# Two transformer blocks in float32 on one core: expert weights given back and loaded by halves for fourteen of sixteen pairs, with three changes of order

## The reference

```
x = x + hybrid_mixer(rmsnorm(x))            # mLSTM branch and spatial gating, one w_in of 10248 columns
x = x + memory_cross_attention(rmsnorm(x), rmsnorm(mem))     # w_xq, w_xkv, w_xo
x = x + hierarchical_moe(rmsnorm(x))        # 32 experts, each token goes to 2:
    hb = silu(xb @ w1[e]) * (xb @ w3[e])    #   w1, w3: 1024 x 512
    y  = hb @ w2[e]                         #   w2: 512 x 1024
x = rmsnorm(x)
# second block: modulation vectors from silu(c) @ w_ada (1024 x 6144), Hyena branch,
# differential attention over x and ctx, SwiGLU with 2816 hidden columns
```

## Time and profile before

| | |
|---|---|
| median of 3 runs | 1299.24 us (1298.53 to 1300.81) |
| the profiled execution | 1300.37 us, span 1298.6 us |
| mean granted TensorE clock | 0.998 of full speed |
| PE busy | 1261.2 us, 97% of the span |
| DVE, ACT, POOL busy | 698.1, 509.3, 102.9 us |
| moved | 362.89 MB, 279 GB/s over the span |

### The profile page before, as it was taken

The page is one execution under the profiler, slowest core; times in us unless marked ns, Lnnn a source line. Parts: engine busy times, 40 slices in busy tenths (PEclk is TensorE's granted clock), DMA queues, the critical chain, the costliest instruction groups (busy, mean ns, idle before and its releaser), DMA issues.

```text
span 1298.6 us, 17828 instructions
## 1 busy us (share of the span) xinstructions
PE 1261.2 (97%) x7053; PEld 887.4 (68%) x7053; DVE 698.1 (54%) x1169; ACT 509.3 (39%) x778; POOL 102.9 (8%) x111
## 2 busy tenths in 40 slices
PE   8999999999999999999999999999999999999998
PEld 7987886976776444444445444449966787899986
DVE  5675668667664323322322222247996868855552
ACT  5556674345244111111111111137344685644442
POOL 6740200200000000000000000000043000000000
PEclk9999999999999999999999999999999999999999
DMA  9654747958876999999999999995416254655440
GB/s 350 240 193 140 251 151 262 371 180 292 308 283 238 402 424 426 426 427 428 429 428 427 425 429 427 427 397 199 154 65 221 104 201 140 194 167 169 184 162 33
DMA packets 103316, 362.89 MB, mean 279 GB/s; under 512 B 4306, under 2 KB 28373, under 8 KB 89600
## 3 DMA queue, kind: packets, MB, share of 16 engines
q1 hardware_dynamic: 99872, 352.60, 70.0%
q0 software_dynamic: 3168, 9.06, 2.2%
q10 hardware_dynamic: 192, 0.06, 0.0%
HBM read 360.65 MB, written 1.05 MB: 279 GB/s over the span
## 4 chain that ended last, share of the span: by engine, by line
PE 85%; DVE 7%; ACT 3%; issue 2%; DMA 1%; POOL 1%; ACTq 0%; DVEq 0%; POOLq 0%
PE bank L544 37%; PE bank L955 17%; PE bank L975 8%; PE bank L929 5%; PE bank L1330 5%; PE bank L1006 3%; DVE ring_parts L1378 2%; PE bank L965 1%; ACT ring_parts L2211 1%; DMA ring<-in_w_xkv 1%; PE bank L633 1%; PE bank L956 1%; PE bank L1170 1%; PE bank L598 1%; PE bank L831 1%
## 5 line engine op out<-in xcount | busy, mean ns | idle before, releaser
L1378 DVE TENSOR_TENSOR ring_parts<-ring,ring_parts 128x1024 fp32r<-128x1024 f32 x202 | 243.6, 1227 | 128.7 <-ACT ring_parts L2211 125.8
L2211 ACT ACTIVATE ring_parts<-ring 128x1024 fp32r<-128x1024 f32 x222 | 230.0, 1057 | 189.6 <-PE bank L544 164.7
L544 PE MATMUL bank<-ring_parts,arena_parts 128*128 128x512 f32 x1056 | 272.3, 393 | 4.1 <-ACT ring_parts L2211 1.5
L544 PEld LDWEIGHTS bank<-ring_parts,arena_parts 128*128 128x128 f32 x1056 | 196.6, 188 | 48.6 <-ACT ring_parts L2211 2.8
L544 PE MATMUL bank<-arena_parts,ring_parts 128*128 128x256 f32 x1504 | 199.4, 285 | 3.0 <-DVE ring_parts L1378 1.8
L955 PE MATMUL bank<-ring,arena 128*64 128x512 f32 x432 | 190.6, 594 | 8.2 <-issue 8.2
L956 PE MATMUL bank<-ring,arena 128*64 128x512 f32 x448 | 197.9, 595 | 0.0
L544 PEld LDWEIGHTS bank<-arena_parts,ring_parts 128*128 128x128 f32 x1504 | 191.4, 193 | 5.1 <-issue 3.3
L955 PEld LDWEIGHTS bank<-ring,arena 128*64 128x64 f32 x432 | 57.5, 137 | 126.7 <-issue 126.7
L2494 ACT ACTIVATE arena<-bank 128x512 f32<-128x512 f32 x32 | 19.1, 597 | 227.4 <-PE bank L956 227.4
L975 PE MATMUL bank<-ring,arena 128*64 128x512 f32 x416 | 106.3, 596 | 0.0
(11 more groups left out here) (411 smaller groups left out, 1502.1 us busy)
## 6 DMA issues: line engine op xcount, KB each, us to landing
ring<-in_w SPq DMA_DIRECT2D x70, 2048.0 KB, 20.9
ring<-in_w_in SPq DMA_DIRECT2D x27, 2048.0 KB, 9.7
ring<-in_w_ada SPq DMA_DIRECT2D x12, 2048.0 KB, 8.7
flank<-in_w SPq DMA_DIRECT2D x12, 2048.0 KB, 21.1
ring<-in_w SPq DMA_DIRECT2D x22, 1024.0 KB, 9.9
ring<-in_w_ffn_gate SPq DMA_DIRECT2D x11, 1024.0 KB, 5.3
ring<-in_w_ffn_up SPq DMA_DIRECT2D x11, 1024.0 KB, 8.0
ring<-in_w_ffn_down SPq DMA_DIRECT2D x5, 2048.0 KB, 7.7
```

What stands on the lines that cost most here:

```text
L544: mm = pe.matmul(ps[:, o:o + width], *pair, start=(o == 0 and kk == 0 and ha + hw == 0), stop=(kk == kn - 1 and (ha, hw) == terms[-1] and ...
L1378: dve.tensor_tensor(low, src, high, ALU.subtract).then_inc(low_ready, 1)
L2211: act.activation(high, src, ACT.Copy).then_inc(high_ready, 1)
```

## The change

Four edits:

1. `HALF_PAIRS` becomes 14: units 7 to 90 are given back and loaded by halves, where it was units 7 to 18.
2. The down product of a pair that is given back by halves (`down_by_rows`, new) has the rows outside: each of the four blocks of rows is read for both halves of the columns before the next, so half the rows have been read in the middle. Both banks are then finished at the end.
3. In the first block's memory keys: `xkv0` is loaded before `ada3`; PE makes `xk0` straight after `ada_sum(1)`, with `ada_sum(2)` between its first two quarters, then `ada_part(3)`, then `xk1` with `ada_sum(3)` between its first two quarters. DVE makes `xkv0`'s first low part amid the products of spatial gating, and the last low parts of the activations (`split_activations(mem_parts, actT, (1, 3))`) ahead of `ada(0)` and `ada(1)`. ACT's list follows.
4. In front of `xq0`: the second tile's transposition (`turn(xT, ..., tiles_of=(1,))`) comes before `ada_part(6)` and `ada_sum(4)`.

```diff
@@ weight_units @@
-    ada_units(0, 4)
-    for j in range(4):
+    ada_units(0, 3)
+    whole("xkv0", cols(w["w_xkv"][0], 0))
+    ada_units(3, 4)
+    for j in range(1, 4):
         whole(f"xkv{j}", cols(w["w_xkv"][0], 512 * j))
@@ -375,7 +377,7 @@
-        HALF_PAIRS = 2
+        HALF_PAIRS = PAIRS - 2
@@ -747,11 +749,18 @@  PE
             ada_part(2)
             ada_sum(1)
+            memory_arrived = halves_split(12)
+
+            def summed(j, arrived=None):
+                def between(q):
+                    if arrived is not None:
+                        arrived(q)
+                    if q == 1:
+                        ada_sum(j)
+                return between
+            split_features("xk0", "xkv0", mem_parts, summed(2, memory_arrived))
             ada_part(3)
-            ada_sum(2)
-            split_features("xk0", "xkv0", mem_parts, halves_split(12))
-            ada_sum(3)
-            split_features("xk1", "xkv1", mem_parts)
+            split_features("xk1", "xkv1", mem_parts, summed(3))
@@ -787,9 +796,9 @@  PE
             ada_part(5)
+            turn(xT, hat2, hats=4, tiles_of=(1,))
             ada_part(6)
             ada_sum(4)
-            turn(xT, hat2, hats=4, tiles_of=(1,))
             ada_sum(5)
@@ -968,6 +977,9 @@  PE, down(n)
                 reach(pe, moe["hid"], 2 * n + 2)
+                if halved(n):
+                    down_by_rows(n, w2u)
+                    return
                 for half in range(2):
...
+            def down_by_rows(n, w2u):
+
+                for half in range(2):
+                    reach(pe, moe[f"low{half}"], n)
+                for k in range(KF):
+                    for half in range(2):
+                        for j in range(2):
+                            mm = pe.matmul(PS[4 + half][j * C:(j + 1) * C, :], hidT[:, j, k, :],
+                                           w2u[j][:, k, half * 512:(half + 1) * 512], start=(k == 0), stop=(k == KF - 1),
+                                           skip_group_check=True)
+                        if k == KF - 1:
+                            mm.then_inc(moe["down"], 1)
+                        elif half and k == KF // 2 - 1:
                             mm.then_inc(moe["half"], 1)
@@ -1587,12 +1612,13 @@  DVE, after each tile of the spatial gating's products
+                if t == 0:
+                    split_low(1)
+
+            split_activations(mem_parts, actT, (1, 3))
             dve.wait_ge(s["G_ready"], 8)
             ada(0)
             ada(1)
-            split_low(1)
-            split_activations(mem_parts, actT, (1, 3))
             split_low(3)
             ada(2)
@@ -2364,10 +2390,11 @@  ACT
             split_activations(memT, mem_parts, actT, (0, 2, 1, 3))
+            split_high(2)
             ada(2)
-            split_high(2)
+            split_high(4)
             ada(3)
-            split_high(2 + 12)
+            split_high(10)
```

More of the change, by code:

```diff
@@ L977, in down @@
                                            skip_group_check=True)
-                        if half and k == KF // 2 - 1 and halved(n):
+                    mm.then_inc(moe["down"], 1)
[9 more added lines that the diff above has]
+                        if k == KF - 1:
+                            mm.then_inc(moe["down"], 1)
+                        elif half and k == KF // 2 - 1:
                             mm.then_inc(moe["half"], 1)
-                    mm.then_inc(moe["down"], 1)
             def down_by_pieces(n):
```

## The result

The changed kernel takes 1311.95 us (median of 4, 1311.50 to 1314.26) beside 1299.84 for the kernel before: 1.0096 of it, 95% interval 1.0081 to 1.0112. The forecast was 1309.2; the median lies at the upper edge of its range. The profiled execution takes 1311.89 us, 11.5 more than the one of before.

A forecast was written before the change was run, and what follows sets the result against it. It took PE, busy 97%, as the bound, with transfers pacing later expert pairs. Expert stage +3.3, memory keys +6.5 and the transposition +0.2 made +10.0 on 1300.37, 1310.4; less 1.1 for the median, 1309.2 us; range 1302 to 1312.

The forecast's parts named there:

- What bounds the stage: Expert stage: later pairs run at the transfers' speed; rival that places were the limit: 1295.6 us, chance 0.06.
- Rate of the halves: Expert stage: halves cost 0.056 us more per unit, +4.0 us for 72 more units.
- The Trainium skill's rule: Expert stage: 1 MiB halves over 128 partitions lose no bandwidth, sum +6.0, 1305.2 us; rival, chance 0.14.
- Order of the halves: Expert stage: first of two units complete 2.5 us later, PE late by 0 to 1.0 at the end: +0.5 us.
- Rows outside: Pair 0's down product: signal 1.8 us earlier closes the idle DMA between 436 and 444 us: -1.2 us.
- Memory keys: First block: PE waits for banks ahead of xk0 and xv0, clock falls after each: 1.6 + 3.2 + 1.7 = +6.5 us.
- The rival by which the banks don't hold PE: Memory keys: no bank waits, the reordering gives -2.0 us; sum +1.5, 1300.7 us; chance 0.11.
- Edit 4: Ahead of xq0: xq0 waits slightly longer for xT1's bank, +0.2 us (-0.4 to 0.6).
- The step from the profiled execution to the median: Whole kernel: the median lies 1.1 us below the profiled execution, taking 1310.4 to 1309.2 us.

The follow-up runs named there:

- e9: Kernel before with only units 7 to 90 given back and loaded by halves, down products as before: 1304.21 us, ratio 1.0034.
- e10: Kernel before with units 19 to 90 each loaded as two 1 MiB transfers by columns, once the whole place is free: 1305.50 us, ratio 1.0036.
- e12: Kernel before with units 19 to 90 loaded by one 2 MiB transfer each, in 8 KB pieces mixing two experts' weights: 1306.13 us, ratio 1.0043.
- e3: Kernel before with only the rows-outside down product, halves for two pairs as before: 1298.58 us, ratio 0.9983.
- e1: Kernel before with units 7 to 90 by halves and the rows-outside down product, nothing else: 1303.71 us, ratio 1.0028.
- e5: Changed kernel with takes renumbered so xk0, xk1, xv0 and adaB3 get the banks of the kernel before: 1305.24 us, ratio 1.0035.
- e4: Kernel before with only the second tile's transposition moved ahead in front of xq0: 1301.18 us, ratio 1.0008.
- e2: Kernel before with only the reordered memory keys: 1307.84 us, ratio 1.0058.
- e6: Kernel before with the reordered memory keys, takes renumbered to keep the old banks: 1300.67 us, ratio 1.0003.
- e7: e6 with xkv0's second low part made earlier, ahead of the activations' last low parts: 1298.81 us against the kernel before, ratio 0.9985.
- e8: e7 with the rows-outside down product in the first two pairs, halves for two pairs as before: 1295.76 us, ratio 0.9961 to the kernel before.

## Where the prediction failed, and what of it held

Its direction and its account of where the time goes held. Two steps of the sum failed. The rate of the halves was mis-sized: +4.0 us forecast, 5.3 to 5.5 measured, which leaves the expert stage at +4.3 for +3.3. And the last step, 1.1 us off from the profiled execution to the median, had nothing to stand on.

- *What bounds the stage* (transfers, not places): right. Share 1.01 throughout, the waits ahead of `up` grew, and earlier issue brings nothing: e9, which issues first halves in the middle of a product where e10 waits for its end, has as long a stage (5.4 us longer than before, e10 5.3 without its stretch at half clock).
- *Rate of the halves, 72 x 0.056 = +4.0:* right in kind, mis-sized; this is the step that failed. 0.46 us a pair is 0.077 a unit, 5.5 for 72; by the stage it is 5.3 (e10) and 5.4 (e9). It was extrapolated from ten landings, read to 0.1 us: over 22.3 us that alone is 1.6 us in 72 units, and I took the middle. That the shorter rows are the cause was no part of the forecast; e12 shows it. The Trainium skill's rule (DMA: Bandwidth & Descriptors, Rules for kernel authors), under which the term would be nothing, is off by a little over 1% here: 421 to 422 GB/s for halves of 1 MiB over 128 partitions, 427 for whole loads.
- *Order of the halves, +0.5:* too much. e9 less e10 leaves 0.1, and that rests on taking 1.7 off for a stretch at half clock. It made up for 0.4 of the term above.
- *Rows outside, -1.2:* right: -1.4 (e3) and -1.2 (e1 beside e9), and where it was put, at 436 us.
- *Memory keys, +6.5:* right. Both banks hold PE (e5), for 3.41 and 3.05 us where 3.4 and 3.2 were forecast, and the clock falls behind both. Of the 7.0 us ahead of the stage, 6.5 are left when e4's 0.5 is taken off, and e2's stage starts 6.5 later. By the medians edit 3 alone costs 0.58%, 7.5 us (5.7 to 9.2). The rival by which the banks don't hold PE counted on a gain of 2.0 (its own sum, 0.1 + 1.5 - 3.5, gives 1.9): e6, with the old banks, gains nothing, since its wait is longer and the clock falls behind it.
- *Edit 4, +0.2:* 0.5 (e4's trace), inside its bounds, and by the bank that was named; by the medians 1.0 (-0.1 to 2.2), which isn't clear of no change.
- *The step from the profiled execution to the median, -1.1:* this failed too, by 1.2. The profiled execution of the changed kernel is its median (1311.89 and 1311.95). The one of before is 1.1 above a median of three; 66 more executions, run beside the experiments, have the median 1300.26, only 0.1 below it. They differ with the clock: the 27 with a mean granted clock of 0.999 or more have the median 1299.47, the other 39 have 1300.66, and the profiled one (0.998) has a stretch at half clock that not all have (below). An offset of that kind isn't handed on to another kernel.

The median is 2.75 us above the forecast: this 1.2, and 1.5 between the profiled executions (11.5 for 10.0), of which 1.0 are in the expert stage, 0.3 in edit 4, 0.4 ahead of everything that was changed and -0.2 behind the stage.

## What to carry to other kernels

Where the transfers set the pace, giving a place back sooner lands nothing sooner (it gained 1.2 to 1.4 us once, at 436 us, where the engines had run out of loads), and cutting rows in two to do it costs bandwidth: look at the landing time beside the time that one load needs by itself. When work is reordered over rotating buffers, write down for each job which earlier job's buffer it now gets and what stands ahead of the reader that frees it; here the numbering alone was worth 6 to 8 us. A step of 1 us from a median of three runs is no term of a sum. A gain can hide in a change that loses: the parts were run alone, and two of them make the fastest kernel.

## What the hardware showed that was not expected

- Rows of 8 KB for 16 KB to each of 128 partitions: 421 to 422 GB/s instead of 427 (e12), with transfers of 2 MiB as with those of 1 MiB (e10).
- Transfers to 64 partitions at a time: 217 GB/s at a share of 1.01, and the stage of 459 us took 791. The share of the DMA engines alone can't tell such a form from a good one.
- The same wait isn't always followed by a fall of the clock. After 1.8 us of idle ahead of `xk0` the kernel before had 3.5 us at 0.51; e3 with the same wait had none, as this stretch shows:

```profile
227.50:231.00 3.50, 3.50 (x32) 3.50 (x31) 3.43 (x6) 1.30 (x2) 0.00 (x0) 1.00 1.05 385
```

Each such stretch is worth 1.7 us (e10 beside e9, above). Other profiled executions have one near 400 us (e4, e7, e12) or between 838 and 853 (e6, e8, e10, e12), so two profiles can differ by this much where no edit reaches. The executions of e6, which has a wait of 1.95 ahead of `xk0`, spread from 1299.16 (mean clock 0.999) to 1302.66 (0.997). A forecast of the median should count such a stretch by how often it comes, which one profile can't tell; why it comes in one execution and not in another stays open.
